# Dense projections of a decoder layer: row normalisation on GpSimd, transposes two steps behind, a third buffer for normalised rows

## The reference, cut to what matters

```python
def rmsnorm(x, g):
    xf = x.astype(jnp.float32)
    y = xf * lax.rsqrt(jnp.mean(xf * xf, axis=-1, keepdims=True) + EPS)
    return (y * g.astype(jnp.float32)).astype(x.dtype)

h = x + mixed @ p['w_out']
kv = (rmsnorm(mem, p['norm_mem']) @ p['w_xkv']).reshape(B, N_MEM, 2, X_HEADS, X_HEAD_DIM)
mkv = jnp.stack([rmsnorm(kv[:, :, 0], p['xk_norm']), kv[:, :, 1]], axis=2)
q = rmsnorm((rmsnorm(h, p['norm_x']) @ p['w_xq']).reshape(B, L, X_HEADS, X_HEAD_DIM), p['xq_norm'])
...
h = h + o @ p['w_xo']
f, new_conv = conv_ffn(rmsnorm(h, p['norm_ffn']), conv_buf, p)
```

## Time and profile before

| | us |
|---|---|
| median of 3 runs | 2240.26 (2239.89 to 2257.68) |
| the profiled execution | 2243.17 |
| its span, first to last instruction | 2241.5 |
| TensorE busy | 1984.5 (89%) |
| VectorE busy | 978.6 (44%) |
| ScalarE busy | 662.8 (30%) |
| GpSimd busy | 260.4 (12%) |

### The profile page before, as it was taken

How to read it: one execution, slowest core, us unless ns; L and a number is a source line. 1 busy time by engine, 2 the same in 40 slices (tenths; PEclk the granted TensorE clock), 3 DMA queues, 4 the chain that set the end, 5 groups by cost and what they waited for, 6 DMA issues and landing times. The chain is left out here.

```text
span 2241.5 us, 32194 instructions
## 1 busy us (share of the span) xinstructions
PE 1984.5 (89%) x12704; PEld 1845.1 (82%) x12704; DVE 978.6 (44%) x2056; ACT 662.8 (30%) x1571; POOL 260.4 (12%) x596
## 2 busy tenths in 40 slices
PE   5899999745698678879989989799999999999997
PEld 5798989634498468879989988799889988899886
DVE  5515445444220543354345023455454455545453
ACT  5324243311311332244444012342132322232221
POOL 2504316034011200000000000000000000000000
PEclk9999999855855589999999589899999999999998
DMA  4101100011054043211032420121111202111102
GB/s 150 55 24 40 53 25 4 4 26 11 8 147 122 19 160 110 85 48 39 1 121 78 122 67 20 48 58 41 46 38 48 58 29 58 29 58 47 40 20 78
DMA packets 135728, 125.24 MB, mean 56 GB/s; under 512 B 15284, under 2 KB 128080, under 8 KB 135602
## 3 DMA queue, kind: packets, MB, share of 16 engines
q1 hardware_dynamic: 129986, 109.28, 16.3%
q0 software_dynamic: 5632, 14.44, 2.0%
HBM read 112.43 MB, written 10.60 MB: 55 GB/s over the span
## 5 line engine op out<-in xcount | busy, mean ns | idle before, releaser
L2382 PE MATMUL bank<-XH,WH 128*128 128x352 f32 x1056 | 343.6, 325 | 0.0
L2382 PE MATMUL bank<-XL,WH 128*128 128x352 f32 x1056 | 339.5, 322 | 0.0
L2382 PE MATMUL bank<-XH,WL 128*128 128x352 f32 x1056 | 339.2, 321 | 0.0
L1866 PE MATMUL bank<-WH,XH 128*128 128x256 f32 (+1 forms) x864 | 251.8, 291 | 18.7 <-DVE WL L1772 18.7
L1866 PE MATMUL bank<-WL,XH 128*128 128x256 f32 (+1 forms) x864 | 248.0, 287 | 0.0
L1866 PE MATMUL bank<-WH,XL 128*128 128x256 f32 (+1 forms) x864 | 246.3, 285 | 0.0
L616 PE MATMUL bank<-WH,XH 128*128 128x256 f32 (+3 forms) x648 | 211.5, 326 | 7.7 <-DVE WL L422 7.7
L2313 DVE TENSOR_TENSOR hres<-hres,bank 128x512 f32<-128x512 f32 (+1 forms) x198 | 135.6, 685 | 176.4 <-PE bank L2406 176.2
L616 PE MATMUL bank<-WL,XH 128*128 128x256 f32 (+3 forms) x648 | 203.6, 314 | 0.0
L616 PE MATMUL bank<-WH,XL 128*128 128x256 f32 (+3 forms) x648 | 202.4, 312 | 0.0
L2382 PEld LDWEIGHTS bank<-XH,WH 128*128 128x128 f32 x1056 | 199.1, 189 | 1.2
(11 more groups left out here) (440 smaller groups left out, 3435.1 us busy)
## 6 DMA issues: line engine op xcount, KB each, us to landing
wstage<-w_up SPq DMA_DIRECT2D x44, 512.0 KB, 5.2
ring<-cache_mem_kv SPq DMA_DIRECT2D x64, 256.0 KB, 2.9
dstage<-w_down POOLq DMA_DIRECT2D x22, 512.0 KB, 3.7
wstage<-w_in SPq DMA_DIRECT2D x10, 1024.0 KB, 5.1
ringS<-cache_kv_dil SPq DMA_DIRECT2D x16, 512.0 KB, 6.8
wstage<-w_xkv SPq DMA_DIRECT2D x8, 1024.0 KB, 5.4
ringS<-cache_kv_dil SPq DMA_DIRECT2D x48, 128.0 KB, 3.2
xin<-x_prompt SPq DMA_DIRECT2D x8, 512.0 KB, 3.5
```

The source lines that it names most:

```text
L1866: ins = nc.tensor.matmul(MM[s % 3][:r, 0:WB], x[:, k, cols], w[:, b % 2, k], start=k == 0 and i == 0, stop=k == KT - 1 and i == 2)
L2382: ins = nc.tensor.matmul(bank[3 * g + j][:, 0:CH], w[:, slot, k, P * g:P * g + P], x[:, k, CH * j:CH * j + CH], start=k == 0 and i == 0, s ...
```

## The change

- The prep's normalisation moves from VectorE to GpSimd. There it is seven instructions in place of five: five small ones (against four), then one pass source x 1/sqrt and a second pass x gain, each over 128x1024. The squares of a `hres` tile go to a spare buffer and no longer into `xn`.
- Prep ends and transposes of normalised rows stand two steps behind the step they belong to (`LAG = 2`) in place of one, on TensorE, ScalarE and VectorE. The two last preps of the first call end at steps 48 and 49, with memory steps between them; those of the second call have no step left between them.
- The two memory preps start at steps 4 and 6 in place of 5 and 7, wait for their own loads only (`ld_m`), and not for the residual add of the step. Their two loads go out in front of the last three loads of x, the other gains behind them.
- Normalised rows rotate through three buffers: `kn[0]`, `kn[1]` and the first 256 columns of `xn[1]`.
- The split of the second weight block stands at step 3 in place of step 1. Waits for the stores of keys and values move from GpSimd's end of the block to SyncE in `block_cross`.

```diff
+    LAG = 2
+    prep_start = {}
     if has_m:
         for p in range(NM):
-            prep_start[2 * p + 5], prep_end[2 * p + 6] = p, [p]
+            prep_start[2 * p + 4] = p
     for s, (st, j, t, b) in enumerate(steps):
         if st in "ox" and j == 3:
             prep_start[s] = h0 + t
-            prep_end[s] = ([h0 + t - 1] if t else []) + ([h0 + t] if t == NT else [])
+    prep_end = {s + LAG: p for s, p in prep_start.items()}
+    turn_at = {s + LAG: n for s, n in norm_at.items()}
+    STEPS = len(steps)
...
+        def normed_rows(n):
+            return kn[:, n % 3] if n % 3 < 2 else xn[:, 1, 0:WB]
...
-            return b + 1 < len(blocks) and t == (0 if st == "m" else 1)
+            return b + 1 < len(blocks) and t == (0 if st == "m" else 1 if b else 3)
...
-                    if t == 5:
-                        load_rest()
+                        for dst, src in S["loadsm"]:
+                            sp.dma_start(dst, src).then_inc(ld_m, 16)
+                load_rest()
...
         @blk.gpsimd
         def _(pool):
+            link = linker(pool, c_pool)
+
+            def prep_norm(p):
+                kind, i = preps[p]
+                n = rows_of(kind, i)
+                pool.wait_ge(p_rt, p + 1)
+                sums, r, tmp = (ssq[:n, x, p:p + 1] for x in range(3))
+                link(nc.gpsimd.tensor_scalar(tmp, sums, -0.5 / D, -0.5 * EPS, ALU.mult, ALU.add))
+                link(nc.gpsimd.tensor_tensor(tmp, tmp, r, ALU.mult))
+                link(nc.gpsimd.tensor_tensor(tmp, tmp, r, ALU.mult))
+                link(nc.gpsimd.tensor_scalar(tmp, tmp, 1.5, None, ALU.add))
+                link(nc.gpsimd.tensor_tensor(r, r, tmp, ALU.mult))
+                if p >= 2:
+                    pool.wait_ge(p_tr, 2 * (p - 1))
+                if has_m and p == h0:
+                    pool.wait_ge(k_st[2], 32)
+                gain = S["gain_m"] if kind == "m" else gain_bc
+                link(nc.gpsimd.tensor_scalar(xn[:n, p % 2], source(kind, i), r, None, ALU.mult))
+                nc.gpsimd.tensor_tensor(xn[:n, p % 2], xn[:n, p % 2], gain[:n], ALU.mult).then_inc(p_n, 1)
...
         @blk.scalar
...
-                if p >= 2:
-                    act.wait_ge(p_tr, 2 * (p - 1))
-                nc.scalar.activation(xn[:n, p % 2], source(kind, i), ACT.Square, accum_out=ssq[:n, 0, p:p + 1])\
-                    .then_inc(c_act, 1)
+                if has_m and p < NM:
+                    act.wait_ge(ld_m, 16 * len(S["loadsm"]))
...
+                out = xn[:n, p % 2] if kind == "m" else spare[:n, 0]
+                nc.scalar.activation(out, source(kind, i), ACT.Square, accum_out=ssq[:n, 0, p:p + 1]).then_inc(c_act, 1)
...
+            for s in range(STEPS + LAG):
+                if s < STEPS:
+                    base(s)
                 if s in prep_start:
-                    act.wait_ge(ev_d, by_dve[s + 1])
+                    if steps[s][0] in "ox" and steps[s][1] == 3:
+                        act.wait_ge(ev_d, by_dve[s + 1])
                     prep_square(prep_start[s])
+                if s in turn_at:
+                    take_transposed(turn_at[s])
+                if s in prep_end:
+                    prep_high(prep_end[s])
...
         @blk.vector
...
-            def prep_norm(p):
-                kind, i = preps[p]
-                n = rows_of(kind, i)
-                dve.wait_ge(p_rt, p + 1)
-                refine_rsqrt(nc, link, ssq[:n, 0, p:p + 1], ssq[:n, 1, p:p + 1], ssq[:n, 2, p:p + 1], D)
-                gain = S["gain_m"] if kind == "m" else gain_bc
-                nc.vector.scalar_tensor_tensor(xn[:n, p % 2], source(kind, i), ssq[:n, 1, p:p + 1],
-                                               gain[:n], ALU.mult, ALU.mult).then_inc(p_n, 1)
...
         @blk.tensor
...
-                if s in norm_at and norm_at[s] >= 1:
-                    transpose_normed(norm_at[s] - 1)
-                for p in prep_end.get(s, []):
-                    prep_transpose(p)
-            if normed:
-                transpose_normed(len(normed) - 1)
+
+            for s in range(STEPS + LAG):
+                if s < STEPS:
+                    base(s)
+                if s in turn_at:
+                    transpose_normed(turn_at[s])
+                if s in prep_end:
+                    prep_transpose(prep_end[s])
```

More of the change, by code:

```diff
@@ L1594, in block_dense, with stores_before @@
         kn = sb("kn", [P, 2, WB])
+        spare = S["mraw"][:] if has_m else sb("spare", [P, 1, D])[:]
+        def normed_rows(n):
+            return kn[:, n % 3] if n % 3 < 2 else xn[:, 1, 0:WB]
+        def stores_before(n):
+            return 16 * sum(r % 3 == n % 3 for r in range(min(n, NM * X)))
         ssq = sb("ssq", [P, 3, len(preps)])
         zr = sb("zr", [P, 3, max(1, len(normed))])
-        ld = sem("ld")
+        ld, ld_m = sem("ld"), sem("ld_m")
         x_ld = [sem(f"x_ld{t}") for t in range(TILES if "o" in stages else 0)]
@@ L1648, in _, with source @@
                     sp.dma_start(wstage[:, :, P * g:P * g + P], up_weights(I)[:, :, g, 0:P]).then_inc(S["w_next"], 16)
+        def source(kind, i):
+            return S["mraw"][:, i] if kind == "m" else hres[:rows(i), i]
         @blk.gpsimd
         def _(pool):
[L1652 to L1658, removed]
+            link = linker(pool, c_pool)
[16 more added lines that the diff above has]
+                nc.gpsimd.tensor_tensor(xn[:n, p % 2], xn[:n, p % 2], gain[:n], ALU.mult).then_inc(p_n, 1)
+            vs = 0
+            for s, (st, j, t, b) in enumerate(steps):
+                if st == "m":
+                    dst = O["mem_kv_p"][0, 0][P * t:P * t + P, j // 4, j % 4]
                     if j < 4:
@@ L1667, in _ @@
                         pool.dma_start(dst, S["Vm"][:, t, WB * (j - 4):WB * (j - 3)]).then_inc(v_st, 16)
[L1668 to L1673, removed]
+                if s in prep_start:
+                    prep_norm(prep_start[s])
         def parts(kind, i, hi):
@@ L1735, in _, with base @@
             split_weights(0)
-            for s, (st, j, t, b) in enumerate(steps):
+            def base(s):
+                st, j, t, b = steps[s]
                 if split_before(s):
                     split_weights(b + 1)
-                if s == 5:
-                    act.wait_ge(ld, n_ld)
                 n_rows = P if st == "m" else rows(t)
@@ L1794, in _, with base @@
             split_weights(0)
-            for s, (st, j, t, b) in enumerate(steps):
+            def base(s):
+                st, j, t, b = steps[s]
                 if split_before(s):
                     split_weights(b + 1)
-                if s == 5:
-                    dve.wait_ge(ld, n_ld)
                 n_rows = P if st == "m" else rows(t)
@@ L1841, in transpose_normed, with base @@
                 for k in range(2):
-                    ins = nc.tensor.transpose(KT_[n % 2][:, P * k:P * k + r], kn[:r, n % 2, P * k:P * k + P],
+                    ins = nc.tensor.transpose(KT_[n % 2][:, P * k:P * k + r], normed_rows(n)[:r, P * k:P * k + P],
                                               ident[:r, :r])
                 ins.then_inc(n_t, 1)
-            for s, (st, j, t, b) in enumerate(steps):
+            def base(s):
+                st, j, t, b = steps[s]
                 r = P if st == "m" else rows(t)
@@ L1914, in _ @@
             sp.dma_start(S["wstage"][:], weight_block(I, "w_xo", 0)).then_inc(S["w_next"], 16)
+            for stored, n in S["stores_m"]:
+                sp.wait_ge(stored, n)
             for j, (kv, b, h) in enumerate(loads):
```

47 lines of the change are left out of this document (23 added, 24 removed).

## The result

The changed kernel took 2257.22 us (median of 20 runs, 2253.28 to 2277.8), the kernel before 2244.19 us (20 runs, 2239.89 to 2263.91): a ratio of 1.007, 95% interval 1.0045 to 1.0095. It is slower by 0.7%. I had forecast 2226.5 us, 0.6% faster, with a range of 2214 to 2243: wrong in sign, and outside the range.

What follows compares the result with a forecast made beforehand. TensorE was taken to set the pace, its waits alone worth gaining, with GpSimd becoming what preps wait for. Terms -2.6 - 1.3 - 1.6 - 2.0 - 5.4 - 1.7 + 0.8 = -13.8 from 2240.3 gave 2226.5 us, range 2214 to 2243.

Steps and rivals of the forecast that it cites:

- The scalar pass reads one tensor ... 1.07 us: GpSimd's source x 1/sqrt pass: between 0.90 and 2.39 us, taken as 1.07, making a prep 5.02 us.
- first rival: GpSimd's scalar pass costs 1.9 us, a prep 5.85 us: 2240.6 us, no change; chance 0.16.
- rival 2: Both GpSimd passes cost 2.39 us, a prep 6.34 us, slower than the old loop: 2248.9 us; chance 0.12.
- 17 us per us of prep: GpSimd's prep price acts 8 times in the first call and 9 in the second.
- Memory tiles: Squares start once both loads land, not behind step 5's add; TensorE's 3.3 us of waits fall to 0.7: -2.6 us.
- Key blocks: Ahead of o1 and o2, waits for normalised keys give way to waits for split weights: -1.3 and -1.6 us.
- Clock: TensorE's granted clock stays up more after the shortened waits at o1 and o2: -2.0 of 3.0 us.
- Tiles of the first call: Nine hres tiles with GpSimd's preps back to back; first q step at 998.2 instead of 1003.57 us: -5.4 us.
- q blocks: The 1.71 us wait at their entry goes with two steps of room: -1.7 us.
- The collision: First call: VectorE's weight split and GpSimd's gain pass meet, gain pass waits; a second, at step 48, costs 2.3 us.
- rivals 3 and 4: 3: VectorE waits behind the gain pass, 2228.8 us, chance 0.08; 4: no collision, prep 4.4 us, 2211.4 us, chance 0.12.
- Second call: Nine preps on GpSimd take 45.2 us, without collision or steps between the last transposes: +0.8 us.

Runs made afterwards that it cites:

- z_after: The changed kernel itself, measured and profiled a second time: 2257.73 us, ratio 1.0053 to the kernel before.
- c_bcast: Changed kernel with GpSimd's scalar pass written as a two-tensor product whose second operand repeats the 1/sqrt column: 2243.42 us, ratio 0.9992 to the kernel before.
- g: Changed kernel with normalisation on VectorE behind the low parts, and ScalarE's high parts ahead of its squares: 2210.32 us, ratio 0.9813 to the kernel before.
- f: Changed kernel with normalisation on VectorE one step after the squares, ScalarE's high parts ahead of its squares: 2211.04 us, ratio 0.982; repeated 2206.88 us, 0.9877.
- i: Changed kernel with normalisation on VectorE ahead of the low parts, and hres prep ends one step behind: 2227.99 us, ratio 0.9923 to the kernel before.
- b: Changed kernel with normalisation on VectorE, behind the low parts of the tile two steps back: 2238.66 us, ratio 1.0015 to the kernel before.
- a: Changed kernel with normalisation back on VectorE, ahead of the low parts of the tile two steps back: 2230.87 us, ratio 0.9934 to the kernel before.
- e: Changed kernel, normalisation still on GpSimd, with hres prep ends one step behind instead of two: 2270.57 us, ratio 1.0122 to the kernel before.
- j_half2: Changed kernel with GpSimd's gain pass first, then 1/sqrt as a repeated operand over 512 columns only: 2226.89 us, ratio 0.9924 to the kernel before.
- d_imm: Changed kernel with GpSimd's scalar pass multiplying by the constant 1.0 in place of the row's 1/sqrt: 2255.93 us, ratio 1.005 to the kernel before.

## Why the prediction was wrong

**The step that failed: "The scalar pass reads one tensor ... 1.07 us", and its upper end, "it costs what the two-tensor pass costs, 2.39".** It measured 2.86 us, above both ends. Even the upper end gives 2248.9 us, and my range stopped at 2243. I had reasoned that an instruction that reads one tensor can't cost more than one that reads two; nothing in the trace said so, and the only GpSimd tensor-scalars in it were 4 columns wide. The row nearest to a pass over one tensor I had overlooked, a square of 2048 columns (both inputs the same; groups by shape of the kernel before):

```profile
L1247 POOL TENSOR_TENSOR sq<-att 128x2048 f32<-128x2048 f32 x3 | 10.8, 3600 | 97.4 <-POOLq L647 82.2 <-DVE st L1315 15.2
```

That is 1.80 us for 1024 columns, by my estimate, about the 1.9 of my first rival. I took the value near the memset's rate, the lower end, on the ground that it differs from the gain pass "in just the second read"; the row nearest in kind was the two-tensor pass, and with that I would have had rival 2, 2248.9 us. It also decided the sign: I had put the turning point at 5.83 us a prep, and it was 6.80. The 17 us per us of prep were right: 1.78 us more for a prep, times 17, is 30 us, and -13.8 + 30 = +16.5 against 13.0 measured.

The Trainium skill, "GPSIMD Engine Reference", section "Engine selection", puts one-input elementwise operations on GpSimd at about line rate, and two-input ones at roughly twice VectorE's time. By the first half the scalar pass would take about 1 us (an estimate), which is where I had put it. The runs disagree: 2.86 us with a per-row operand, 2.78 with a constant, both above the 2.34 of the two-input form.

**Memory tiles (-2.6): right, and undersized.** No wait is left where I had kept 0.7, so 3.3 us of waits are gone. The loads landed earlier than I had put them: the first squares started 12.0 us after the first matmul, against the 16.5 of my step.

```profile
815.98 1.06 ACT L1746 ACTIVATE xnmoq<-mraw 128x1024 f32<-128x1024 f32 x1 [2.32 <-DMA gain_m<-norm_mem]
```

**Key blocks (-1.3, -1.6): right.** The waits for keys have gone and the split weights wait in their place, 2.30 and 1.89 us, where I had put 1.9 and 1.8. **Clock (-2.0): right in kind.** The granted clock stays at its upper level (2.4 GHz) over the stretches that follow, against 0.76 and 0.50 before; behind the 2.69 us wait in front of o3 it still falls (0.57 over 929 to 933 us). Windows (us, then busy PE, PEld, DVE, ACT, POOL, clock, DMA, GB/s):

```profile
848.00:852.00 4.00, 3.55 (x30) 3.55 (x31) 2.83 (x12) 0.63 (x3) 1.08 (x2) 1.00 0.58 162
888.00:892.00 4.00, 3.45 (x29) 3.45 (x30) 2.83 (x12) 0.61 (x4) 1.08 (x2) 1.00 0.48 153
```

Between the first matmuls of o2 and o3 lie 40.5 us after and 42.1 before, with the same wait in front of o3 (2.69 and 2.70 us): 1.7 us that no removed wait explains, near the 2.0 of that row. Up to o3 the four terms together had -7.5; -9.8 was measured.

**Tiles of the first call (-5.4).** With eight preps 1.78 us dearer this term becomes +8.8, and with -1.7 for the q blocks and -7.5 for what lies ahead I would have had -0.4 at the second call. It was -3.9; 2.3 of the 3.5 lie ahead of o3.

**The collision (rivals 3 and 4).** It is real, and either side can lose it. The first one fell otherwise than forecast: the split met the scalar pass, not the gain pass (last section). Of the second, timelines of VectorE and GpSimd in z_after, where VectorE's split came first; then of another profiled execution of the same kernel (the one taken with the result), where GpSimd came first by 0.04 us:

```profile
987.76 2.29 DVE L1807 TENSOR_TENSOR WL<-wstage,WH 128x2048 fp32r<-128x2048 f32 x1 [1.11 <-ACT WH L1735]
...
988.04 4.21 POOL L1689 TENSOR_TENSOR xnmoq<-xnmoq,gain_bc 128x1024 f32<-128x1024 f32 x1
```

```profile
1006.45 4.47 DVE L1807 TENSOR_TENSOR WL<-wstage,WH 128x2048 fp32r<-128x2048 f32 x1 [1.11 <-ACT WH L1735]
...
1006.41 2.36 POOL L1689 TENSOR_TENSOR xnmoq<-xnmoq,gain_bc 128x1024 f32<-128x1024 f32 x1
```

The one that starts second is longer by nearly what the other still has to run: 4.47 is 2.29 + 2.18, with 2.32 to run; 4.21 is 2.37 + 1.84, with 2.01 to run. So the Trainium skill, "SBUF — State Buffer", section "SBUF: two separate sides" (whoever starts first holds the shared ports for its whole instruction), agrees with these two pairs. In time it decided little: the two executions take 644.4 us (GpSimd late) and 642.1 us (VectorE late) from the first dense matmul to the first of the feed-forward.

**Second call (+0.8): right once priced.** From its first matmul to the first of the feed-forward it took 134.5 us before and 151.2 after, +16.7; my step with the measured price gives 0.8 + 9 x 1.78 = 16.8. Nine preps on GpSimd, one behind the other, were the right model.

**Rivals.** Rival 2's mechanism is what happened (GpSimd takes the place of the old loop and is slower than it), at a higher price than it had. Rival 1's price is that of c_bcast (5.79 us a prep against 5.85), and its time too: level with before.

What I had not asked is whether VectorE could have kept the work. Its normalisation was not too long for the loop: with ScalarE's high parts ahead of its squares (g, f) the tiles take 4.17 and 3.73 us on the same engine. f is 35 us below before; 13.7 us of that, by i's trace, are the change's part outside the tiles, the rest is the order.

## What to carry to other kernels

A pass that moves to another engine is priced by a row of the same instruction form at the same width on that engine; where there is none, the bound on top is not "the form that does more", and the price that turns the sign belongs in the range. Before moving work off an engine that idles half the time, follow the loop around its waits. Put what others wait for ahead of what only a later step needs (here ScalarE's high parts ahead of its squares, 25 us between the traces of b and g); then, if the engine still waits inside a step for what another has just begun, let it do the tile of the step before (4 us, g to f). More steps of room gained nothing while that loop was closed (a against i), but were needed once a slow engine had to be kept fed (e, 13 us).

## What the runs showed of the hardware that I had not expected

- On GpSimd, a 128x1024 float32 tensor-scalar took 2.86 us with a per-row operand and 2.78 us with a constant; a two-tensor instruction 2.34 to 2.40 us; a two-tensor instruction whose second operand repeats one column 1.89 us, and 1.04 us over 512 columns (c_bcast, j_half2). The form that reads least was the dearest.
- Against the scalar pass VectorE's split lost much less than against the gain pass, 0.6 us instead of 2.2 (timelines of VectorE and GpSimd in z_after; 0.6 too in the profile taken with the result, 0.2 with d_imm's constant):

```profile
937.36 2.86 POOL L1688 TENSOR_SCALAR xnmoq<-hres,ssqmoq 128x1024 f32<-128x1024 f32 x1
...
937.70 2.92 DVE L1807 TENSOR_TENSOR WL<-wstage,WH 128x2048 fp32r<-128x2048 f32 x1 [3.59 <-ACT WH L1735]
```

  Waiting for the end of the 2.86 us pass would have made it 2.29 + 2.52. In c_bcast, where the same product is a two-tensor instruction, the split started 0.36 us behind it and took 3.67 us, 1.38 longer, with 1.53 us of the pass to run: that form holds VectorE up, the tensor-scalar form hardly. Why was not tried.
